# Causal attention with both heads' scores issued together, probabilities scaled in place and then transposed

## The reference, cut to what matters

```python
def _masked_softmax(s, mask):
    s = jnp.where(mask, s.astype(jnp.float32), -jnp.inf)
    m = jnp.max(s, axis=-1, keepdims=True)
    m = jnp.where(jnp.isfinite(m), m, 0.0)
    p = jnp.exp(s - m)
    return p / jnp.maximum(jnp.sum(p, axis=-1, keepdims=True), 1e-30)
...
return gc[..., 0:1] * oc + gc[..., 1:2] * osl + gc[..., 2:3] * ow
```

## Time and profile before

| | us |
|---|---|
| median of 3 runs | 3285.07 |
| lowest and highest run | 3270.03, 3287.79 |
| the profiled execution, time | 3267.99 |
| its span | 3266.2 |
| PE busy in it | 2748.4 (84%) |
| DVE busy in it | 1703.7 (52%) |
| ACT busy in it | 1079.5 (33%) |

### The profile page before, as it was taken

The page is one execution under the profiler, slowest core; times in us unless marked ns, Lnnn a source line. Parts: engine busy times, 40 slices in busy tenths (PEclk is TensorE's granted clock), DMA queues, the critical chain, the costliest instruction groups (busy, mean ns, idle before and its releaser), DMA issues. The chain is left out here.

```text
span 3266.2 us, 41926 instructions
## 1 busy us (share of the span) xinstructions
PE 2748.4 (84%) x15966; PEld 2125.7 (65%) x15966; DVE 1703.7 (52%) x2643; ACT 1079.5 (33%) x1788; POOL 91.9 (3%) x101
## 2 busy tenths in 40 slices
PE   7979899756658999998968999957799847599998
PEld 4634887645346788786637888846666636478886
DVE  3535222677554588637976877342224362454432
ACT  3322101354212555324334554221124210245531
POOL 0034000000000000000000000000000000000000
PEclk9989999966878999999988999978769967699999
DMA  8723132001014233421112333222100100223332
GB/s 294 248 81 129 52 84 58 13 4 47 7 52 135 65 97 96 112 62 52 51 30 61 102 97 95 80 58 76 52 7 1 47 1 2 65 78 96 96 98 71
DMA packets 374147, 240.99 MB, mean 74 GB/s; under 512 B 8048, under 2 KB 345840, under 8 KB 374000
## 3 DMA queue, kind: packets, MB, share of 16 engines
q1 hardware_dynamic: 374000, 238.96, 24.6%
HBM read 236.31 MB, written 2.10 MB: 73 GB/s over the span
## 5 line engine op out<-in xcount | busy, mean ns | idle before, releaser
L1086 DVE SCALAR_TENSOR_TENSOR ffn_acc<-ffn_pad,cols_sb,ffn_acc 128x512 f32<-128x512 f32 x380 | 263.7, 746 | 32.6 <-ACT ffn_acc L1013 32.6
L223 PE MATMUL bank<-ffn_x_high,pre_high 128*128 128x512 f32 x528 | 212.2, 402 | 14.2 <-DVE ffn_x_low L475 10.7
L224 PE MATMUL bank<-ffn_x_low,pre_high 128*128 128x512 f32 x528 | 210.6, 399 | 0.0
L225 PE MATMUL bank<-ffn_x_high,pre_low 128*128 128x512 f32 x528 | 210.6, 399 | 0.0
L223 PE MATMUL bank<-ffn_x_high,ffn_w_high 128*128 128x512 f32 x528 | 205.5, 389 | 0.0
L225 PE MATMUL bank<-ffn_x_high,ffn_w_low 128*128 128x512 f32 x528 | 205.5, 389 | 0.0
L224 PE MATMUL bank<-ffn_x_low,ffn_w_high 128*128 128x512 f32 x528 | 205.4, 389 | 0.0
L223 PE MATMUL bank<-ffn_h_high,ffn_down_w_high 128*128 128x512 f32 x480 | 190.3, 397 | 0.0
L224 PE MATMUL bank<-ffn_h_low,ffn_down_w_high 128*128 128x512 f32 x480 | 189.6, 395 | 0.0
L225 PE MATMUL bank<-ffn_h_high,ffn_down_w_low 128*128 128x512 f32 x480 | 188.7, 393 | 0.0
L1307 DVE SCALAR_TENSOR_TENSOR conf_u<-conf_pad,cols_sb,conf_u 128x512 f32<-128x512 f32 x162 | 121.8, 752 | 16.9 <-ACT conf_u L1274 11.7
(11 more groups left out here) (734 smaller groups left out, 6388.0 us busy)
## 6 DMA issues: line engine op xcount, KB each, us to landing
ada_ring<-in_ada_w SPq DMA_DIRECT2D x48, 1024.0 KB, 7.0
pre_ring<-in_ffn_w_up SPq DMA_DIRECT2D x88, 512.0 KB, 3.9
pre_ring<-in_ffn_w_in SPq DMA_DIRECT2D x44, 512.0 KB, 3.9
ffn_down_ring<-in_ffn_w_down SPq DMA_DIRECT2D x28, 704.0 KB, 4.7
ffn_down_ring<-in_ffn_w_out SPq DMA_DIRECT2D x14, 704.0 KB, 4.5
pre_ring<-in_conf_w SPq DMA_DIRECT2D x18, 512.0 KB, 5.0
f_ring<-in_mix_w_in SPq DMA_DIRECT2D x32, 256.0 KB, 3.0
mix_out_ring<-in_mix_w_out SPq DMA_DIRECT2D x16, 512.0 KB, 3.9
```

The lines of the kernel that those rows point to most:

```text
L223: pe.matmul(bank, weights[0], acts[0], start=start, stop=False)
L224: pe.matmul(bank, weights[0], acts[1], start=False, stop=False)
L225: return pe.matmul(bank, weights[1], acts[0], start=False, stop=stop)
L1086: dve.scalar_tensor_tensor(out=dst, in0=src, scalar=conv_w(2 * i + j, n), in1=dst, op0=ALU.mult, op1=ALU.add).then_inc(tapped[j], 1)
```

## The change

1. `scores` handles a head pair: the products of head 0 (rows 0 to 63) and head 1 (rows 64 to 127) follow each other, into two of four banks (0 to 3). Only head 0 gets its mask by the second product on PE, after both. Head 1's mask is added by DVE in the bank, 128 columns, before its maximum.
2. `diag` goes. `finish` multiplies the probabilities in place in SBUF by 1/sum, over the whole width of the unit.
3. `turn` is PE's transpose against the identity instead of a product with `diag`, into banks 4 and 5. The values of all tiles share bank 6.
4. The order: PE issues the scores of two head pairs, then four 512-wide products of constants into bank 7 that nothing reads, and then for each q the transposes of both units of head pair q, the scores of head pair q + 2, and what follows (`after`). DVE reduces both units of q and then finishes q - 1. ACT takes the exponentials of head pair q and then copies out head pair q - 2.

```diff
-    depth, lag = 6, 4
+    n_q = n_u // 2
+    depth, lag = 6, 2
...
+        def by_pe(e):
+            return e == 0
...
-            def scores(u):
-                p, t, e = units[u]
+            def scores(q):
+                p, t, _ = units[2 * q]
                 branch = pairs[p][1]
...
+                if q >= 2:
+                    pe.wait_ge(exp_done, 2 * (q - 1))
+                for e in range(2):
+                    rows = slice(HD * e, HD * e + HD)
+                    mm = pe.matmul(score_bank(2 * q + e)[:, 0:width(2 * q)], branch.q[rows, t * P:(t + 1) * P],
+                                   branch.k[rows, 0:width(2 * q)], start=True, stop=not by_pe(e))
+                    if not by_pe(e):
+                        mm.then_inc(scored[e], 1)
+                for e in range(2):
+                    if by_pe(e):
+                        pe.matmul(score_bank(2 * q + e)[:, t * P:(t + 1) * P], ident[:, :], masked[:, :], start=False, stop=True)\
+                          .then_inc(scored[e], 1)
...
-                    mm = pe.matmul(banks[3 + u % 2][:, n * P:(n + 1) * P], prob[:, u % depth, n * P:(n + 1) * P],
-                                   diag[:, u % depth, :], start=True, stop=True)
+                    mm = pe.transpose(banks[4 + u % 2][:, n * P:(n + 1) * P], prob[:, u % depth, n * P:(n + 1) * P],
+                                      core.const("ident"))
...
-            for s in range(n_u + lag):
-                if s < n_u:
-                    scores(s)
-                if s >= lag:
-                    turn(s - lag)
-                    after(s - lag)
+            for q in range(lag):
+                scores(q)
+            for n in range(4):
+                pe.matmul(banks[7][:, :], core.const("ident"), core.const_sb[:, 0:TT, :].rearrange("p n q -> p (n q)"),
+                          start=True, stop=True)
+            for q in range(n_q):
+                for e in range(2):
+                    turn(2 * q + e)
+                if q + lag < n_q:
+                    scores(q + lag)
+                after(2 * q + 1)
...
-                    if u >= depth:
-                        dve.wait_ge(turned, u - depth + 1)
-                    dve.tensor_scalar(diag[:, u % depth, :], core.const("ident"), total[:, u:u + 1], None, ALU.mult)\
-                       .then_inc(scaled, 1)
+                    dve.tensor_scalar(probs(u), probs(u), total[:, u:u + 1], None, ALU.mult).then_inc(scaled, 1)
...
-            for u in range(n_u):
-                dve.wait_ge(scored, u + 1)
-                dve.tensor_reduce(top[:, u:u + 1], banks[u % 3][:, 0:width(u)], AX_X, ALU.max, negate=True).then_inc(top_done, 1)
-                if u >= 3 and u % 2 == 1:
-                    finish((u - 3) // 2)
...
+            for q in range(n_q):
+                t = units[2 * q][1]
+                for e in range(2):
+                    u = 2 * q + e
+                    dve.wait_ge(scored[e], q + 1)
+                    if not by_pe(e):
+                        last = score_bank(u)[:, t * P:(t + 1) * P]
+                        dve.tensor_tensor(last, last, core.const("neg_since"), ALU.add).then_inc(masked_out, 1)
+                        dve.wait_ge(masked_out, q + 1)
+                    dve.tensor_reduce(top[:, u:u + 1], score_bank(u)[:, 0:width(u)], AX_X, ALU.max, negate=True).then_inc(top_done, 1)
+                if q:
+                    finish(q - 1)
```

More of the change, by code:

```diff
@@ L2719, in causal_attention @@
     n_u, n_t = len(units), len(tiles)
[L2720 removed]
+    n_q = n_u // 2
+    depth, lag = 6, 2
     sq = core.in_arena("att_sq", [P, 2, SEQ], F32, 12 * 1024)
     with core.room(att_p=[P, depth, SEQ], att_pt=[P, 2, 2, TT, SEQ], att_top=[P, n_u], att_sum=[P, n_u],
[L2723 removed]
+                   att_root=[P, 2 * TT * n_t]) as (prob, prob_t, top, total, root), \
             core.split_room(att_mask=[P, P]) as ((ident, masked),), \
[L2725 removed]
+            core.stage("masks_in", "scored0", "scored1", "masked_out", "top_done", "exp_done", "guarded", "inverted", "gated", "scaled", "turned", "taken",
                        "summed", "lifted", "squared", "counted", "var_done", "root_done", "root_inverted", "spread_done", "normed") as (
[L2727 removed]
+                block, masks_in, scored0, scored1, masked_out, top_done, exp_done, guarded, inverted, gated, scaled, turned, taken, summed, lifted,
                 squared, counted, var_done, root_done, root_inverted, spread_done, normed):
@@ L2733, in probs, with score_bank @@
             return prob[:, u % depth, 0:width(u)]
+        def score_bank(u):
+            return banks[u % 4]
+        def by_pe(e):
+            return e == 0
+        scored = [scored0, scored1]
         @block.tensor
         def _(pe):
-            def scores(u):
-                p, t, e = units[u]
+            def scores(q):
+                p, t, _ = units[2 * q]
                 branch = pairs[p][1]
[L2740 to L2746, removed]
+                if q >= 2:
[10 more added lines that the diff above has]
+                          .then_inc(scored[e], 1)
             def turn(u):
@@ L2758, in values @@
                 n_tile, branch = pairs[p]
-                bank = banks[5 + n_tile % 2]
+                bank = banks[6]
                 first = p == 0 or pairs[p - 1][0] != n_tile
@@ L2762, in values @@
                 pe.wait_ge(taken, UNITS * (p + 1))
-                if first and n_tile >= 2:
-                    pe.wait_ge(lifted, n_tile - 1)
+                if first and n_tile >= 1:
+                    pe.wait_ge(lifted, n_tile)
                 if first and cmp_pair is not None:
@@ L2817, in take @@
                 act.activation(prob_t[:, p % 2, e, 0:t + 1, t * P:(t + 1) * P],
-                               banks[3 + u % 2][:, 0:width(u)].rearrange("k (n q) -> k n q", q=P), ACT.Copy).then_inc(taken, 1)
+                               banks[4 + u % 2][:, 0:width(u)].rearrange("k (n q) -> k n q", q=P), ACT.Copy).then_inc(taken, 1)
             def square(n_tile):
@@ L2824, in square @@
                 act.activation(sq[:, n_tile % 2, :], mix[:, tiles[n_tile][0], :], ACT.Square).then_inc(squared, 1)
[L2826 to L2835, removed]
+            for q in range(n_q + lag):
+                if q < n_q:
+                    for u in (2 * q, 2 * q + 1):
+                        act.wait_ge(top_done, u + 1)
+                        if u >= depth:
+                            act.wait_ge(turned, u - depth + 1)
+                        act.activation(probs(u), score_bank(u)[:, 0:width(u)], ACT.Exp, bias=top[:, u:u + 1],
+                                       accum_out=total[:, u:u + 1]).then_inc(exp_done, 1)
+                if q >= lag:
+                    for u in (2 * (q - lag), 2 * (q - lag) + 1):
+                        take(u)
                     if u % UNITS == 7 and u // UNITS - 1 in ends:
```

8 lines of the change are left out of this document (4 added, 4 removed).

## The result

| | before | after |
|---|---|---|
| median of 20 executions | 3285.77 us (3265.60 to 3302.73) | 3301.03 us (3294.74 to 3305.18) |
| profiled execution | 3268 us, span 3266.2 | 3298.92 us, span 3297.1 |
| ratio after to before | | 1.0056, 95% interval 1.0040 to 1.0072 |

The change makes the kernel slower by 0.6%. The direction is the forecast's, the size is not: 3301 against 3325 us.

What follows compares the result with a forecast made beforehand. PE's queue was taken to bound the old kernel; after the change, a circle of waits through PE and DVE. The stage goes from 163 to 205 us, 3285 + 42 = 3327, rounded to 3325 us; range 3268 to 3365.

Steps and rivals of the forecast that it cites:

- PE's work per branch: Attention stage on PE: falls from 15.3 to 9.8 us per branch at 2.4 GHz, and PE no longer sets the pace.
- the first step: Scores of both heads on PE: three passes' time, between bounds of two and four; 0.80 us per head pair at 2.4 GHz.
- The prediction's own sign for this: Wrong if head 0's mask product starts less than 0.7 of four passes after the first score pass.
- rounds of 4.6 and 6.4: Time per head pair in the attention stage: 4.6 us at 2.4 GHz, 6.4 us at 1.2 GHz.
- three in five at 1.2 GHz: Share of head pairs at the low clock: mean 5.7 us per head pair, stage 205 us.
- the second step: Sum for the whole kernel: the stage's 42 us over 163 added to the median, 3285 + 42 = 3327, rounded to 3325 us.
- The ring: Scores, maxima, DVE's finish and transposes follow one another in a circle: 4.6 us per head pair, 166 us for 36.
- The clock: Attention stage: raised by constant products, falls soon after, rises at value products and falls again; stage 205 us.
- Granted clock 0.6 to 0.8 over the stage: Sign for the forecast in the attention stage; wrong on the clock if 1.00 from start to end, or 0.50.
- The clock stays at 2.4 GHz: Rival, chance 0.23: attention stage keeps the full clock, 3285 + 5 = 3290 us, within 0.5%.
- Transposes don't hold the clock up: Rival, chance 0.12: only scores and value products count, nearly everything runs at 1.2 GHz, +69 us, 3354 us.
- The ring is not closed: Rival, chance 0.15, faster: at PE's wait for scaled, below 4.0 us per head pair; stage 115 to 125 us, halfway 3262.

Runs made afterwards that it cites:

- experiment 1: Changed kernel with PE issuing the scores of head pair q + 2 before the transposes of q, no longer behind them: 3231.06 us, 0.9875 of before.
- experiment 4: Changed kernel with both heads' scores taken from head 0's rows, so both products share one row group: 3350.71 us.
- experiment 8: Kernel before, unchanged, run and profiled again (3270.07 to 3287.05 us), and once with four constant products behind its third score tile (3274.43 us).
- after_filler: The kernel of experiment 2: changed kernel plus two unread 384-column constant products behind each head pair's scores: 3272.27 us, 0.9997 of before.
- Experiment 2: Changed kernel plus two 384-column constant products, which nothing reads, behind each head pair's scores: 3272.27 us, 0.9997 of before.
- experiment 7: Changed kernel with a product with the constant identity, two passes per block, in place of the transpose: 3324.20 us.
- experiment 3: Changed kernel without its four constant products ahead of the loop: 3301.16 us.
- before_warm: Kernel before with the four constant products issued behind the third score tile, nothing else: 3274.43 us, 1.0006 of before.
- before_turns_twice: Kernel before with in-place scaling and each transpose issued twice into the same place, two passes per block: median 3283.92 us.
- after_swap: The kernel of experiment 1: changed kernel with scores of head pair q + 2 issued before the transposes of q: 3231.06 us, 0.9875 of before.
- before_fourth: Kernel before, unchanged, one more execution with its profile: 3287.05 us.
- before_again: Kernel before, unchanged, run for a second profile: 3270.07 us.
- before_turns: Kernel before with in-place scaling and PE transposes with the constant identity, old order, banks and masks: 3281.27 us, 0.9992 of before.

## Why the prediction was right in direction and wrong in size

**PE's work per branch.** The passes are as forecast: 180 transposes, each 0.109 us at 2.4 GHz. That PE would no longer set the pace is right too; experiment 1 shows that it was the order.

**Where the first step failed: three passes for the scores of two heads.** "I take three, since head 1's first pass can run beside head 0's second". They take the time of two: a 512-wide pair reaches its mask product 1.06 us after its start (2499.70 to 2500.76), and one tile took 1.06 before; experiment 4 shows that the rows do it. The prediction's own sign for this came true: it was to be wrong if the mask started less than 0.7 of four passes after the first one, 1.20 us at 512 columns. The promise that the Trainium skill makes in TensorEngine Tiling (Array Packing), "Theoretical Speedup", held in full here; the order of starts and ends that TensorE: Matmul & The Clock Gate of the Trainium skill gives in "The mechanism", read as three passes, gave the wrong sum. The pass that I charged too much is 0.27 us per head pair at 2.4 GHz and 0.53 at 1.2. The forecast's rounds of 4.6 and 6.4 become 4.33 and 5.87, its mean over three in five at 1.2 GHz 5.25 instead of 5.7, and the stretch 36 x 5.25 = 189 us. It measured 192.5. So the step cost 16 of the 205 us forecast, and other terms missed by 3.5 the other way.

**Where the second step failed: 42 us added to the median.** "So on the median it is 3285 + 42 = 3327". The 42 were counted against a stretch of 163 us, which belongs to an execution of 3268; an execution of before at the median has a stretch of 181 (experiment 8). The 17 us between the two lie inside the very work that the change replaces, so they had to be left out: 3268 + 42 = 3310, or 3285 + 205 - 181 = 3309. With the scores' step mended as well it is 3268 + 26 = 3294, and after measured 3301. The two steps together give 16 + 17 = 33 us too much; the remaining 9 (24 was the miss) were too little: 3.5 in the stretch, 1.1 outside it, 2.1 between after's profiled execution and its median, and 2 by rounding 3327 to 3325. After's own executions lie within 10 us, since its branches rise and fall in each one.

**The ring.** Right in kind, and nearly in each DVE term. The profile's groups of after:

```profile
L2892 DVE TENSOR_TENSOR bank<-bank,const_sb 128x128 f32<-128x128 f32 x36 | 10.4, 290 | 0.0
L2877 DVE TENSOR_SCALAR att_p<-att_p,att_sum 128x512 f32<-128x512 f32 x18 | 7.9, 484 | 0.3
L2877 DVE TENSOR_SCALAR att_p<-att_p,att_sum 128x128 f32<-128x128 f32 x18 | 4.3, 284 | 0.3
```

The mask addition was taken as 284 ns and the scaling as 284 to 481. At a clock of 0.95 (`after_filler`) the round measured 4.66 us; the mended forecast is 4.33 at 2.4 GHz throughout, and 4.45 with a tenth of the time at 5.87, so the round was some 5% longer than the mended sum, if the constant products themselves cost nothing there.

**The clock.** "Granted clock 0.6 to 0.8 over the stage" was right (0.70), and so was the picture of a rise at value products and a fall behind them. Some luck is in the 189 us. The forecast has three in five head pairs at 1.2 GHz, which is 68% of its time; a clock of 0.70 is 60%. With that share the mended rounds give 36 x 5.15 = 185 us, so the rounds were longer than forecast by about 4%, and the larger share at 1.2 GHz hid half of it. Windows of after show the fall behind the constant products as well (0.83 from 2390 to 2400 us, 0.50 from 2410 to 2420). Experiment 2 shows that work in the ring's pauses brings the clock back, experiment 7 that a second pass per block doesn't (0.73). The nearly 40 us at 1.2 GHz at the start of before are another matter: in the ring the constant products didn't shorten that part (experiment 3), in the old order they did (`before_warm`).

**The rivals.** *The clock stays at 2.4 GHz* didn't happen; `after_filler` comes nearest to it, 3272 us, about no change. *Transposes don't hold the clock up* is out: by the Trainium skill (TensorE: Matmul & The Clock Gate, "Part 4: PE-mode transpose") the full clock doesn't engage for them, but the trace of `before_turns_twice`, with nothing but transposes in that place, has 0.83 against 0.77 to 0.87 for before; the two disagree, and the measurement decides. *The ring is not closed* is out for the order as written and true for `after_swap`, whose 121.8 us lie inside the 115 to 125 given for it.

## What to carry to other kernels

When calls are fused or regrouped, follow one round through all engines: if the only work that PE has queued between "what DVE waits for" and "what waits for DVE" is gone, no saving on PE counts. Here the order of two calls was worth 71 us, where the whole change moved the median by 15. Before a difference is added to a median, ask in which part of the program the executions of the old kernel differ; if it is the part that is replaced, that spread goes with it. Two fp32 products on separate halves of the array's rows and into separate banks, issued back to back, took the time of one here.

## What the runs showed of the hardware that was not expected

- Two fp32 products of 64 rows each, on separate rows and into separate banks: 1.06 us for both from the first pass to the mask at 512 columns and 2.4 GHz, as for one; on the same rows 3.71 us instead of 2.00 at 1.2 GHz.
- The clock can fall to 1.2 GHz with no pause of PE in the records: in `before_fourth` PE was busy for all of the two branches that fell, about 5 us behind their value products (0.61 and 0.62), and `before_again`, PE busy 16.1 us of 16.3 and 16.1 in the same two, kept 1.00. `before_turns` fell in most branches (0.68 over the stretch, PE busy 98% of it).
- Fewer passes can cost the clock: with one transpose per block it was 0.68 over the stretch, with two 0.83, and the kernel with twice as many took about as long (3274 to 3289 us against 3274 to 3287).
- Four 512-wide products of constants at the start raised the clock from 0.50 to 1.00 for the 20 us that followed, in the order that leaves PE work to do, and not in the one with the ring.
